# Sparse layer of a four-layer network: compression keys and key sets computed by rows with the values and then turned, and every engine's list in a new order

## The chip, the cores and the metric

One core of one Trainium2 chip runs the whole kernel. The metric is the device time of one execution in microseconds (us). The time before is 866.23 us, the median of 3 runs (866.14 to 866.57).

## The reference, cut to what matters

The reference is a whole network on one sequence of 256 rows of 1024 numbers, all float32: an even layer (top-k sparse attention and retention), an odd layer (differential and low-rank attention), a "sparse" layer with compressed, selected and window attention, and a layer with block attention over shared keys; the last two are each followed by a convolutional feed-forward network. The change touches the arithmetic of the sparse layer alone:

```
q, kc, vc, ks, vs, kw, vw, g, qm = split_cols(x @ a_w_in, sizes)   # 768, 6 x 64, 36, 256 columns
k_cmp = nsa_compress(heads(kc), pe_k, w1_k, w2_k)   # 15 blocks of 32 rows, through a small network
v_cmp = nsa_compress(heads(vc), pe_v, w1_v, w2_v)
gates = sigmoid(g)
o_main = nsa_attention(q, k_cmp, v_cmp, ks, vs, kw, vw, gates, rel_bias)
o_mem = memory_attention(qm, mem, w_mem_kv)
x = layer_norm(ALPHA * x + concat(o_main, o_mem) @ w_out, ln1_g, ln1_b)
```

## The kernel before, in words

**Precision.** Float32 accuracy is kept with the faster fp32r form: each weight and each input is cut into a high part (`whi`, `thi`) and the rest (`wlo`, `tlo`), and a product is three matmuls: high by high, low by high, high by low. ScalarE (ACT) makes the high part of a weight unit (L762), VectorE (DVE) the rest (L769). Of weight units that are split there are 262, of at most 128x1024 numbers, loaded in a fixed order by SyncE (SP, L736) into 4 raw buffers and split into 6 pairs of high and low buffers; a unit's `hi` waits until the unit six before it has been used for the last time.

**Two kinds of linear.** A "tile" (`pe_tile` L787, `pe_tile_low` L803) has 128 weight columns as the stationary operand and all 256 rows as the moving one, so its result comes out turned (columns on the partitions). For most names the high pass takes 512 moving columns at once (L797: rows' high and low parts side by side); for `e_idx` and `a_c` it takes two matmuls of 256 (L800, L801). The low pass is L809. A "chunk" (`pe_chunk` L847, `pe_chunk_low` L866) has 128 rows of the input as the stationary operand (q is 0 or 1) and the weight columns as the moving one, so its result comes out by rows: L861 (high by high), L864 (low by high), L872 (high by low). Both kinds end in one of PSUM's 8 banks, handed out in turn (`in_turn`, L629); in the sparse layer linears use banks 0 and 1 in turn. `p.fill` lets TensorE (PE) wait until the bank's last reader is done.

**The sparse layer's first linears.** `a_v` is a chunk linear of 164 columns (128 of values, 36 of gates) in 2 weight units: 8 slices of the contraction, 2 row blocks, 3 passes, so 48 matmuls of 164 columns. DVE copies the values (`vsw`, L2059), ACT takes the exponential of the gates (`gte`, L2028). `a_c` is two tiles of 128 columns (keys and values for compression; the two key sets): 2 x 24 matmuls of 256 columns. ACT copies each tile in four pieces (L2019 to L2023). Then follow the tiles `a_qm` and `a_q` and the compression (`w1`, L1964, `comp1`, `comp3`, `cmps`, `cmp`, `cmpt`).

**Attention.** Each group of heads goes through `log` (scores, L1062, into banks 4 and 5, both of them for every group), `mask` (DVE, L1179 or L1175, which empties the banks), `exp` (ACT, L1191), `mul` (DVE, L1210), `turn` (transposes, L1071), `pt` (ACT and DVE copies), and `val` (probabilities by values: L1119, and L1101 for the differential groups; in the sparse layer L1112 comes first). Most `log` steps use 64 of the 128 partitions of the stationary side, with two halves of the array side by side; `val` steps other than the differential ones use 64 of the array's columns, again two halves side by side. The `log` steps of the groups l0 to l2 use the full array. Below, "half-array steps" means the first two; `score`, `rets`, `brow`, `w1` and `cmps` (L1603, L1614 to L1633, L1964, L1997) likewise use a part of the array.

**Other steps on PE.** `T` turns the layer's input (L905), `proj` and `plow` are the output projection (L973), `mix` L932, `uq` and `ukv` L1789 to L1813, `jt` L2151, and `up`, `ulow`, `down` in the feed-forward network L2161, L2169, L2189.

**What sets the order.** The table `ORDER` (L241) holds for each of seven sections (start, even, odd, nsa, ffn0, moba, ffn1) one list of steps for each of PE, ACT, DVE and POOL, written out in the file. Each engine runs its list strictly in order; semaphores do the rest. `hi n` on ACT and `lo n` on DVE split the next n weight units.

Of the kernel before, what the change touches and what calls it, by code (L numbers as in the profile page):

```python
# [235 lines left out]
def listed(text):  # L236
# [21 lines left out]
        T 1 1 0, T 1 1 1, chunk e_av 0 0, clow e_av 0 0, chunk e_av 1 0, clow e_av 1 0, chunk e_av 0 1, clow e_av 0 1, chunk e_av 1 1,  # L258
        clow e_av 1 1, chunk e_av 2 0, clow e_av 2 0, chunk e_av 2 1, clow e_av 2 1, chunk e_av 3 0, chunk e_av 3 1, clow e_av 3 0,
        clow e_av 3 1, tile e_idx 0, tile e_idx 1, tile e_idx 2, tlow e_idx 0, tlow e_idx 1, tlow e_idx 2, tile e_rot 0, tlow e_rot 0,  # L260
        tile e_rot 1, tlow e_rot 1, iw, score 0, tile e_rot 2, tlow e_rot 2, score 1, tile e_rot 3, tlow e_rot 3, chunk e_bv 0 0,
        chunk e_bv 1 0, clow e_bv 0 0, clow e_bv 1 0, chunk e_bv 0 1, clow e_bv 0 1, tile e_q 0, chunk e_bv 2 0, chunk e_bv 1 1,
        chunk e_bv 2 1, clow e_bv 1 1, clow e_bv 2 0, clow e_bv 2 1, chunk e_bv 3 0, chunk e_bv 3 1, clow e_bv 3 0, tlow e_q 0,
        clow e_bv 3 1, tile e_q 1, tlow e_q 1, tile e_q 2, tlow e_q 2, rets 0, brow, tile e_q 3, tlow e_q 3, tile e_k 0, tlow e_k 0,
        rets 2, retv 0, retv 1, tile e_k 1, tlow e_k 1, retv 2, retv 3, tile e_k 2, tile e_k 3, tlow e_k 2, tlow e_k 3, tile e_ag 0,
        tile e_ag 1, log d0, tlow e_ag 0, tlow e_ag 1, tile e_ag 2, log d1, chunk e_bg 0 0, tile e_ag 3, tlow e_ag 2, tlow e_ag 3,
        clow e_bg 0 0, chunk e_bg 1 0, clow e_bg 1 0, turn d0 0, turn d0 1, log d2, chunk e_bg 2 0, chunk e_bg 3 0, chunk e_bg 0 1,
        clow e_bg 0 1, chunk e_bg 1 1, turn d1 0, turn d1 1, clow e_bg 1 1, val d0, chunk e_bg 2 1, chunk e_bg 3 1, val d1, turn d2 0,
        turn d2 1, clow e_bg 2 0, clow e_bg 3 0, clow e_bg 2 1, clow e_bg 3 1, val d2, proj e 0 1, proj e 1 1, proj e 0 0, plow e 0 0,
# [2 lines left out]
        proj e 4 1, proj e 5 1, plow e 4 1, plow e 5 1, proj e 6 1, plow e 6 1, proj e 7 1 0, T 3 0 0, proj e 7 1 1, T 3 0 1"""),
        act=listed("""
        T 1 1 0, T 1 1 1, hi 4, chunk e_av 0, hi 1, chunk e_av 1, rot 0, hi 3, tile e_idx 0, hi 1, tile e_idx 1, tile e_idx 2, hi 2,
        rot 1, half e_rot 0, half e_rot 1, relu 0 0, relu 0 1, hi 3, half e_rot 2, relu 1 0, relu 1 1, half e_rot 3, hi 3, chunk e_bv 0,
        hi 1, chunk e_bv 1, hi 2, half e_q 0, half e_q 1, half e_q 2, hi 2, half e_q 3, half e_k 0, half e_k 1, hi 3, half e_k 2,
        half e_k 3, hi 3, half e_ag 0, half e_ag 1, exp d0 0, exp d0 1, hi 1, half e_ag 2, half e_ag 3, exp d1 0, exp d1 1, hi 1, pt d0,
        exp d2 0, exp d2 1, silu e, brow, pt d1, out d0, out d1, pt d2, chunk e_bg 0, hi 1, chunk e_bg 1, hi 1, out d2, hi 3, mix e 2,
        mix e 3, hi 3, sq post0 0 0, sq post0 0 1, hi 1, sq pre1 0 0, sq pre1 0 1, hi 2, sq post0 1 0, T 3 0 0, sq post0 1 1, T 3 0 1,
        hi 1, sq pre1 1 0, sq pre1 1 1, hi 1"""),  # L280
        dve=listed("""
        T 1 1 0, T 1 1 1, lo 2, rt 0 0, rt 0 1, lo 2, rt 0 2, lo 1, rt 1 0, lo 4, rt 1 1, lo 1, rt 1 2, lo 1, iw, sum e_rot 0, score 0, rt 2 0,
        sum e_rot 1, lo 3, sum e_rot 2, sum e_rot 3, score 1, top 0, top 1, lo 3, top 2, top 3, top 4, lo 1, sum e_q 0, top 5, lo 1,
        sum e_q 1, sum e_q 2, dec 0, top 6, dec 1, lo 2, sum e_k 0, top 7, dec 2, sum e_q 3, dec 3, topmask, lo 1, sum e_k 1, lo 2,
        rstat 0, sum e_k 2, sum e_k 3, rstat 1, rout 0, mask d0 0, brow, mask d0 1, sum e_ag 0, sum e_ag 1, lo 3, mask d1 0, mul d0,
        mask d1 1, rout 1, sum e_ag 2, sum e_ag 3, mask d2 0, mask d2 1, pt d0, mul d1, lo 1, mul d2, pt d1, gated d0, lo 1, outlo d0,
        gated d1, pt d2, outlo d1, lo 1, gated d2, lo 1, gate e 0, gate e 1, outlo d2, lo 4, mix e 2, mix e 3, lo 3, gain post0 0 0,
        gain post0 0 1, xw e 0 0, xw e 0 1, lo 1, row pre1 0 0, row pre1 0 1, gain post0 1 0, T 3 0 0, gain post0 1 1,
        T 3 0 1, xw e 1 0, xw e 1 1, lo 1, row pre1 1 0, row pre1 1 1, lo 1"""),
        pool=listed("""  # L290
        rope 0, rope 1, rope 2, rope 3, rroot 0, rroot 1, rms post0 0, rms pre1 0, rms post0 1, rms pre1 1""")),
    odd=dict(
        pe=listed("""
        chunk o_lora 0 0, clow o_lora 0 0, chunk o_lora 1 0, chunk o_v 0 0, clow o_lora 1 0, chunk o_lora 2 0,
        chunk o_lora 3 0, clow o_lora 2 0, T 3 1 0, chunk o_v 1 0, T 3 1 1, chunk o_lora 0 1, clow o_lora 0 1, chunk o_lora 1 1,
# [2142 lines left out]
```

## Time and profile before

| | before |
|---|---|
| median of 3 runs | 866.23 us |
| span of the profiled execution | 864.6 us |
| PE busy | 855.4 us, 99% |
| PE weight loads busy | 725.5 us, 84% |
| DVE busy | 671.9 us, 78% |
| ACT busy | 489.5 us, 57% |
| POOL busy | 40.3 us, 5% |
| DMA | 155.12 MB, mean 179 GB/s |

The profile has no time of its own for the profiled execution other than its span, from the first to the last instruction; the rest of a run's time lies around the span. PE matmuls overlap, so a busy PE is not yet a PE at its best: the useful number is the distance from the start of one step to the start of the next, which the chain of waits gives (start, length, engine and line, count).

### The profile page before, as it was taken

The page shows a single profiled execution, that of the slowest core. Times are in us where ns is not written, and L with a number is a line of the kernel's source. Part 1 is how long each engine was busy: PE and PEld are TensorE (multiplying, and loading weights), DVE is VectorE, ACT ScalarE, POOL GpSimd, SP SyncE. Part 2 cuts the span into 40 slices and gives each one's busy share as a digit, 9 for nine tenths or more (in the row PEclk, how much of TensorE's full clock was granted, in tenths as well). Part 3 has the DMA queues.
Part 4 walks back from the last instruction along what each step waited for, and adds up shares of the span by engine and source line. Part 5 has one row for each costly group of instructions (what it writes and reads, how often), then busy time and mean ns, then how long its engine had stood idle before and what let it go on. Part 6 is the DMA issues. An engine that isn't in the chain of part 4 may idle for free.

```text
span 864.6 us, 13438 instructions
## 1 busy us (share of the span) xinstructions
PE 855.4 (99%) x5062; PEld 725.5 (84%) x5062; DVE 671.9 (78%) x1238; ACT 489.5 (57%) x905; POOL 40.3 (5%) x72
## 2 busy tenths in 40 slices
PE   9999999999999999999999999999999999999997
PEld 7888888888888878788888888888888888888885
DVE  4889887868886788988776867887768787677876
ACT  5584375668775776655555445545664565544541
POOL 0105000110001100000000000000000000000000
PEclk9999999999999999999999999999999999999999
DMA  9775526467436861235566556537344456566641
GB/s 328 287 240 150 167 80 194 137 221 222 167 99 228 268 219 49 77 111 179 172 202 212 174 193 228 188 131 251 115 159 146 146 195 221 169 220 213 216 155 49
DMA packets 46748, 155.12 MB, mean 179 GB/s; under 512 B 5500, under 2 KB 8668, under 8 KB 46684
## 3 DMA queue, kind: packets, MB, share of 16 engines
q1 hardware_dynamic: 41408, 141.39, 48.9%
q10 hardware_dynamic: 5276, 12.88, 4.9%
q8 instruction: 40, 0.66, 0.3%
q14 instruction: 24, 0.20, 0.1%
HBM read 152.38 MB, written 1.34 MB: 178 GB/s over the span
## 4 chain that ended last, share of the span: by engine, by line
PE 97%; DVE 1%; ACT 1%; DMA 0%; issue 0%; SPq 0%; POOL 0%; DVEq 0%
PE ps L2161 17%; PE ps L2189 14%; PE ps L797 12%; PE ps L973 10%; PE ps L2169 9%; PE ps L809 6%; PE ps L861 5%; PE ps L872 4%; PE ps L864 4%; PE ps L1062 4%; PE ps L1119 3%; PE ps L1071 3%; PE ps L905 1%; PE ps L800 1%; PE ps L801 1%; DMA raw<-in_ws 0%
## 5 line engine op out<-in xcount | busy, mean ns | idle before, releaser
L769 DVE TENSOR_TENSOR wlo<-raw,whi 128x1024 fp32r<-128x1024 f32 (+1 forms) x262 | 311.1, 1216 | 56.6 <-ACT whi L762 55.3
L762 ACT ACTIVATE whi<-raw 128x1024 fp32r<-128x1024 f32 x261 | 266.6, 1049 | 115.9 <-DMA raw<-in_ws 37.1
L2161 PE MATMUL ps<-t,whi 128*128 128x512 f32 x640 | 156.1, 391 | 0.0
L2161 PEld LDWEIGHTS ps<-t,whi 128*128 128x128 f32 x640 | 117.7, 188 | 22.8
L797 PE MATMUL ps<-t,whi 128*128 128x512 f32 x432 | 109.3, 397 | 0.0
L2189 PE MATMUL ps<-whi,r 128*128 128x512 f32 x352 | 95.4, 391 | 0.0
L797 PEld LDWEIGHTS ps<-t,whi 128*128 128x128 f32 x432 | 78.2, 188 | 17.3 <-issue 1.8
L2169 PEld LDWEIGHTS ps<-t,wlo 128*128 128x128 f32 x640 | 84.7, 191 | 4.7
L2169 PE MATMUL ps<-t,wlo 128*128 128x256 f32 x640 | 86.4, 283 | 0.0
L2189 PEld LDWEIGHTS ps<-whi,r 128*128 128x128 f32 x352 | 64.6, 188 | 12.2
L809 PEld LDWEIGHTS ps<-t,wlo 128*128 128x128 f32 (+1 forms) x472 | 62.5, 189 | 4.2 <-issue 0.3
L809 PE MATMUL ps<-t,wlo 128*128 128x256 f32 (+1 forms) x472 | 64.8, 283 | 0.0
L861 PE MATMUL ps<-whi,t 128*128 128x512 f32 (+3 forms) x192 | 56.2, 379 | 0.8 <-ACT whi L760 0.6
L2189 PE MATMUL ps<-wlo,r 128*128 128x512 f32 x176 | 54.9, 390 | 0.0
L864 PE MATMUL ps<-whi,t 128*128 128x512 f32 (+3 forms) x192 | 54.3, 371 | 0.1
L872 PE MATMUL ps<-wlo,t 128*128 128x512 f32 (+3 forms) x192 | 49.7, 371 | 0.0
L1191 ACT ACTIVATE sm<-sm,stat 128x128 f32<-128x128 f32 (+1 forms) x92 | 40.4, 442 | 5.6 <-DVE stat L1179 5.6
L825 ACT ACTIVATE arena<-ps 128x256 f32<-128x256 f32 x50 | 18.5, 380 | 41.9 <-PE ps L809 41.6
L861 PEld LDWEIGHTS ps<-whi,t 128*128 128x128 f32 x192 | 33.1, 188 | 8.1 <-issue 1.3
L864 PEld LDWEIGHTS ps<-whi,t 128*128 128x128 f32 x192 | 34.2, 188 | 6.8 <-DVE t L917 1.0
L2189 PEld LDWEIGHTS ps<-wlo,r 128*128 128x128 f32 x176 | 33.0, 188 | 7.0
L872 PEld LDWEIGHTS ps<-wlo,t 128*128 128x128 f32 x192 | 33.7, 188 | 5.8 <-issue 0.3
(277 smaller groups left out, 1149.4 us busy)
## 6 DMA issues: line engine op xcount, KB each, us to landing
raw<-in_ws SPq DMA_DIRECT2D x251, 512.0 KB, 4.5
vecs<-in_vecs ACTq DMA_DIRECT2D x12, 512.0 KB, 4.6
arena<-in_ws ACTq DMA_DIRECT2D x5, 512.0 KB, 7.5
raw<-in_ws SPq DMA_DIRECT2D x8, 256.0 KB, 5.6
raw<-in_ws SPq DMA_DIRECT2D x4, 416.0 KB, 4.3
tb<-brow ACTq DMA_DIRECT2D x8, 192.0 KB, 4.3
rows<-in_mem SPq DMA_DIRECT2D x4, 256.0 KB, 5.2
x<-in_x SPq DMA_DIRECT2D x1, 1024.0 KB, 7.6
```

What stands on the lines that cost most here:

```text
L762: a.i.activation(whi[:, j % NSPLIT, 0:n], raw[:, j % NRAW, 0:n], ACT.Copy).then_inc(*a.sig("hi", u))
L769: d.i.tensor_tensor(wlo[:, j % NSPLIT, 0:n], raw[:, j % NRAW, 0:n], whi[:, j % NSPLIT, 0:n].bitcast(F), ALU.subtract).then_inc(*d.sig("lo" ...
L797: p.i.matmul(ps[:, b, :], wh[:, k, :], t2[:, k, :], start=k == 0, stop=False)
L809: mm = p.i.matmul(ps[0:m, b, 0:T], wl[:, k, :], thi[:, k, :], start=False, stop=k == 7)
L861: p.i.matmul(chunk_out(name, b, n), thi[:, k0 + kl, q * P:q * P + P], wh[:, kl, :], start=k == 0 and kl == 0, stop=False)
L864: p.i.matmul(chunk_out(name, b, n), tlo[:, k0 + kl, q * P:q * P + P], wh[:, kl, :], start=False, stop=False)
L872: mm = p.i.matmul(chunk_out(name, b, n), thi[:, k0 + kl, q * P:q * P + P], wl[:, kl, :], start=False, stop=final and kl == nk - 1)
L973: mm = p.i.matmul(ps[:, 2 * q + z, :], x_, w_[:, 0, 512 * z:512 * z + 512], start=n == 0 and y == 0, stop=y == 2 and n + 1 in (8, add), sk ...
L1191: ex = a.i.activation(o, i, ACT.Exp, bias=g.m[:, s * n + c:s * n + c + 1], scale=1.0 if g.kind == "mem" else -1.0, accum_out=g.l[:, l:l + 1])
L2161: p.i.matmul(ps[:, b, :], wh[:, k, :], t2[:, k, :], start=k == 0, stop=False)
L2169: mm = p.i.matmul(ps[:, b, 0:T], wl[:, k, :], thi[:, k, :], start=False, stop=k == 7)
L2189: mm = p.i.matmul(ps[:, 2 * q + n, :], g_, w_[:, 0, 512 * n:512 * n + 512], start=False, stop=final and y == 2, skip_group_check=True)
```

## The change

The 256 columns of `a_c` join the 164 of `a_v`: one chunk linear of 420 columns in 4 weight units of 840 numbers a partition. ACT copies the 256 new columns of each row block to `crows` (which lies in `hrow`), and PE turns them with four transposes of 128x128 into bank 0, where the four-piece copies find them. All lists are in a new order. SP loads the same bytes in the same number of units.

```diff
-    chunk("a_v", a, span(960, 64) + span(1088, 64) + span(1152, 36))
-    tiles("a_c", a, span(768, 128) + span(896, 64) + span(1024, 64))
+    chunk("a_v", a, span(960, 64) + span(1088, 64) + span(1152, 36) + span(768, 128) + span(896, 64) + span(1024, 64))
...
+    N["crows"] = N["hrow"].rearrange("p (q n) -> p q n", q=2)
...
-                   a_v=164, b_v0=512, b_v1=256, f_in0_0=512, f_in1_0=512)
+                   a_v=420, b_v0=512, b_v1=256, f_in0_0=512, f_in1_0=512)
...
-    in_turn(*both("a_v"), *each("a_c"), *each("a_qm"), *each("a_q"), n=2)
+    in_turn(*both("a_v"), "a_c", *each("a_qm"), *each("a_q"), n=2)
...
+            elif name == "a_v":
+                p.fill(b, ("ev", "a_v", q), ("crows", q))
...
+            elif what == "crows":
+                b = BANK["a_c"]
+                p.fill(b, ("ev", "a_c", 0), ("ev", "a_c", 1))
+                for q in range(2):
+                    p.wait_ge("crows", q)
+                    for t in range(2):
+                        mm = p.i.transpose(ps[:, b, t * T + q * P:t * T + q * P + P], N["crows"][:, q, t * P:t * P + P], ident[:, :])
+                mm.then_inc(*p.sig("c_turned", 0))
...
-                pv = ps[:, BANK["a_c", t], 0:T]
-                a.wait_ge("lin", "a_c", t)
+                pv = ps[:, BANK["a_c"], t * T:t * T + T]
+                a.wait_ge("c_turned", 0)
...
+            elif what == "crows":
+                q = k[0]
+                a.wait_ge("evd", "a_v", q)
+                a.i.activation(N["crows"][:, q, :], ps[:, BANK["a_v", q], 164:420], ACT.Copy).then_inc(*a.sig("crows", q))
```

Of the lists, those parts that the prediction speaks of. PE, start:

```diff
-        warm 6 7, T 0 0 0, warm 3 7, chunk mv 0 0, T 0 1 0, clow mv 0 0, chunk mv 0 1, clow mv 0 1, T 0 0 1, T 0 1 1, chunk mv 1 0, chunk mv 1 1,
+        warm 6 7, T 0 0 0, warm 3 7, chunk mv 0 0, T 0 1 0, clow mv 0 0, T 0 0 1, chunk mv 1 0, chunk mv 0 1, clow mv 0 1,
+        T 0 1 1, clow mv 1 0, chunk mv 2 0, chunk mv 1 1, chunk mv 3 0, chunk mv 3 1, chunk mv 2 1, clow mv 1 1, clow mv 2 0,
+        clow mv 3 0, clow mv 2 1, clow mv 3 1, tile mk0 0, tile mk0 1, tlow mk0 0, tlow mk0 1, tile mk1 0, tlow mk1 0,
```

PE, sparse layer (nsa), in its first half:

```diff
-        chunk a_v 0 0, clow a_v 0 0, chunk a_v 1 0, clow a_v 1 0, T 5 1 0, T 5 1 1, chunk a_v 0 1, chunk a_v 1 1, clow a_v 0 1,
-        clow a_v 1 1, tile a_c 0, tlow a_c 0, tile a_c 1, tlow a_c 1, tile a_qm 0, tlow a_qm 0, tile a_qm 1, tlow a_qm 1, w1 k 0, w1 k 1,
-        w1 k 2, log m0, tile a_q 0, tile a_q 1, log m1, tlow a_q 0, tlow a_q 1, turn m0 0, turn m0 1, w1 k 3, w1 v 0, w1 v 1, w1 v 2,
-        w1 v 3, log n0, tile a_q 2, tlow a_q 2, log n1, comp1, tile a_q 3, tlow a_q 3, turn m1 0, turn m1 1, log n2, val m0, comp3,
-        tile a_q 4, tlow a_q 4, val m1, turn n0 0, turn n0 1, tile a_q 5, tlow a_q 5, turn n1 0, log n3, cmps, proj a 0 0, cmp,
...
+        chunk a_v 0 0, chunk a_v 1 0, clow a_v 0 0, clow a_v 1 0, T 5 1 0, chunk a_v 3 0, chunk a_v 2 0, T 5 1 1, chunk a_v 0 1,
+        clow a_v 2 0, clow a_v 3 0, chunk a_v 3 1, chunk a_v 1 1, clow a_v 0 1, chunk a_v 2 1, clow a_v 1 1, clow a_v 2 1,
+        clow a_v 3 1, crows, tile a_qm 0, tlow a_qm 0, tile a_qm 1, tlow a_qm 1, tile a_q 0, tlow a_q 0, log m0, w1 k 0, w1 k 1,
+        w1 k 2, w1 k 3, w1 v 0, w1 v 1, log m1, tile a_q 1, tlow a_q 1, turn m0 1, tile a_q 2, turn m0 0, tlow a_q 2, log n0,
+        val m0, w1 v 2, w1 v 3, log n1, turn m1 1, turn m1 0, comp1, log n2, tile a_q 3, tlow a_q 3, tile a_q 4, turn n0 0,
+        tlow a_q 4, turn n0 1, tile a_q 5, log n3, tlow a_q 5, comp3, log n4, val m1, cmps, turn n1 0, turn n1 1, cmp,
+        proj a 0 0, turn n2 0, plow a 0 0, proj a 1 0, plow a 1 0, proj a 0 1, log n5, turn n2 1, cmpt 0, proj a 1 1, val n0,
+        log n6, turn n3 1, cmpt 1, proj a 2 0, plow a 0 1, val n1, log n7, plow a 2 0, plow a 1 1, turn n3 0, val n2, turn n4 0,
+        proj a 2 1, plow a 2 1, turn n4 1, val n3, log n8, proj a 3 0, proj a 4 0, proj a 5 0, turn n5 0, val n4, turn n5 1,
```

ACT and DVE, the opening of the sparse layer; PE in the odd layer, in the first feed-forward network and in the last layer's attention (parts):

```diff
-        T 5 1 0, T 5 1 1, gte 0, hi 2, gte 1, hi 1, tile a_c 0, hi 1, tile a_c 1, hi 3, half a_qm 0, half a_qm 1, w1load 4, w1load 5,
+        T 5 1 0, hi 1, T 5 1 1, hi 1, gte 0, hi 1, w1load 4, crows 0, crows 1, gte 1, tile a_c 0, tile a_c 1, hi 1, half a_qm 0,
+        hi 3, half a_qm 1, w1load 5, half a_q 0, exp m0 0, exp m0 1, hi 1, w1load 6, w1load 7, exp m1 0, hi 1, half a_q 1,
...
+        T 5 1 0, lo 1, T 5 1 1, lo 1, vsw 0, lo 1, vsw 1, lo 2, sum a_qm 0, sum a_qm 1, blocks, mask m0 0, mask m0 1, lo 2,
...
-        chunk o_lora 3 0, clow o_lora 2 0, T 3 1 0, chunk o_v 1 0, T 3 1 1, chunk o_lora 0 1, clow o_lora 0 1, chunk o_lora 1 1,
+        clow o_lora 2 0, chunk o_v 1 0, T 3 1 0, T 3 1 1, clow o_lora 3 0, clow o_v 0 0, chunk o_lora 0 1, chunk o_lora 3 1,
...
-        chunk f_in0_0 2 1, clow f_in0_0 2 1, chunk f_in0_0 3 1, clow f_in0_0 3 1, jt 0, up 0 1 0, up 0 1 1, ulow 0 1 0, ulow 0 1 1,
+        chunk f_in0_0 2 1, clow f_in0_0 0 1, clow f_in0_0 2 1, clow f_in0_0 3 1, up 0 1 0, jt 0, ulow 0 1 0, up 0 1 1,
...
+        clow b_v1 0 0, tile b_q 3, chunk b_v1 0 1, tlow b_q 3, chunk b_v1 1 1, chunk b_v1 1 0, clow b_v1 0 1, tile b_k 4,
+        clow b_v1 1 0, log g3, val m3, log g4, clow b_v1 1 1, tile b_q 4, tlow b_q 4, turn g2 1, turn g2 0, tlow b_k 4,
+        tile b_k 5, tlow b_k 5, turn g3 0, tile b_q 5, turn g4 1, turn g3 1, tlow b_q 5, val g2, log g5, val g3, turn g4 0,
+        proj b 0 1, proj b 0 0, proj b 1 0, plow b 0 0, val g4, log g6, turn g5 0, plow b 1 0, proj b 2 0, turn g5 1,
```

## Rows read from the trace of the kernel before

**Rows 1.** The page: span, busy time, granted clock, chain by engine.

```profile
span 864.6 us, 13438 instructions
PE 855.4 (99%) x5062; PEld 725.5 (84%) x5062; DVE 671.9 (78%) x1238; ACT 489.5 (57%) x905; POOL 40.3 (5%) x72
...
PEclk9999999999999999999999999999999999999999
...
PE 97%; DVE 1%; ACT 1%; DMA 0%; issue 0%; SPq 0%; POOL 0%; DVEq 0%
```

**Rows 2.** Chain of waits, opening of the sparse layer: start us, length us, what, count.

```profile
282.41 0.63 PE ps L861 x6
...
285.06 0.64 PE ps L905 x4
...
286.48 1.03 PE ps L861 x6
...
289.57 0.15 PE ps L800
...
295.37 1.84 PE ps L797 x8
297.20 0.95 PE ps L809 x8
```

**Rows 3.** Chain of waits, odd layer: matmuls of 416 columns.

```profile
171.51 0.38 PE ps L861 x2
```

**Rows 4.** Timelines of DVE and ACT, opening of the sparse layer: start us, length us, instruction.

```profile
289.61 0.29 DVE L2059 COPY arena<-ps 128x128 f32<-128x128 f32 x1 [0.76 <-PE ps L872]
...
295.40 0.38 ACT L2022 ACTIVATE arena<-ps 64x256 f32<-64x256 f32 x1 [0.24 <-PE ps L809]
...
299.97 0.38 ACT L825 ACTIVATE arena<-ps 128x256 f32<-128x256 f32 x1
```

**Rows 5.** DMA view, issues by tensor: count, size of one, median us to landing.

```profile
rows<-in_ws ACTq DMA_DIRECT2D x2, 512.0 KB, 5.4
```

**Rows 6.** Chain of waits: half-array steps and what follows them.

```profile
239.75 1.16 PE ps L1062 x16
...
310.48 0.87 PE ps L1071 x8
...
324.64 1.02 PE ps L1119 x16
...
330.58 1.02 PE ps L1071 x8
...
334.84 1.09 PE ps L1062 x16
...
339.37 1.06 PE ps L1062 x8
340.43 3.44 PE ps L973 x14
```

**Rows 7.** Chain of waits, feed-forward network, at its step `jt 0`.

```profile
399.60 0.61 ACT arena L2226
...
400.25 0.66 PE ps L2151 x4
```

**Rows 8.** Timeline of PE, odd layer, at the step `T 3 1 0`.

```profile
168.29 0.66 PE L905 MATMUL ps<-ident,rows 128*128 128x128 f32 x4 [0.16 <-DVE rows L1352]
```

**Rows 9.** Chain of waits at the start, and ACT's timeline of the same stretch.

```profile
7.04 0.50 PE ps L861
...
12.45 0.47 PE ps L861 x2
...
19.27 1.06 ACT L762 ACTIVATE whi<-raw 128x1024 fp32r<-128x1024 f32 x1 [1.06 <-DMA raw<-in_ws]
```

**Rows 10.** Timeline of DVE: first and last `mask` instruction of the group n3 (16 in all).

```profile
335.98 0.29 DVE L1179 CUSTOM_DVE_ANT_0 sm<-ps,tb 128x128 f32<-128x128 f32 x1 [0.70 <-PE ps L1062]
...
337.68 0.09 DVE L1179 DVE_READ_ACCUMULATOR2_ANT stat<- 128x1 f32 x1
```

More of the change, by code:

```diff
@@ L257 @@
         pe=listed("""
[L258 to L269, printed above, removed]
@@ L275 @@
[L275 to L278, printed above, removed]
@@ L285 @@
[L285 to L288, printed above, removed]
@@ new lines @@
+        tile e_ag 2, tlow e_ag 1, tlow e_ag 2, log d1, tile e_ag 3, chunk e_bg 0 0, turn d0 0, tlow e_ag 3, clow e_bg 0 0,
+        turn d0 1, chunk e_bg 2 0, chunk e_bg 1 0, chunk e_bg 0 1, val d0, log d2, turn d1 1, turn d1 0, chunk e_bg 3 1,
+        chunk e_bg 3 0, clow e_bg 2 0, chunk e_bg 1 1, val d1, clow e_bg 1 0, clow e_bg 3 0, turn d2 0, turn d2 1,
+        clow e_bg 1 1, clow e_bg 0 1, chunk e_bg 2 1, clow e_bg 2 1, clow e_bg 3 1, val d2, proj e 0 0, plow e 0 0, mix e 2,
+        proj e 3 0, proj e 0 1, plow e 0 1, proj e 4 0, mix e 3, proj e 5 0, proj e 2 0, proj e 1 1, proj e 6 0, plow e 3 0,
@@ L290 @@
+        xw e 1 1, lo 2, row pre1 1 0, row pre1 1 1"""),
         pool=listed("""
@@ L298 @@
-        chunk o_v 3 1, l2 0, l2 1, tile o_q 0, clow o_v 3 1, tlow o_q 0, tile o_q 1, tlow o_q 1, tile o_q 2, tlow o_q 2, tile o_q 3,
-        tlow o_q 3, uq 0, uq 1, uq 2, uq 3, ukv 0, ukv 1, ukv 2, ukv 3, log l0, tile o_dg 0, tlow o_dg 0,
-        log l1, tile o_dg 1, tile o_dg 2, turn l0 0, turn l0 1, log l2, tlow o_dg 1, tlow o_dg 2, tile o_dg 3, tlow o_dg 3, tile o_k 0,
-        tlow o_k 0, val l0, turn l1 0, turn l1 1, tile o_k 1, tlow o_k 1, tile o_k 2, turn l2 0, turn l2 1, tlow o_k 2, val l1,
@@ L321 @@
[L321 to L324 removed]
+        chunk o_lora 0 0, chunk o_lora 1 0, clow o_lora 0 0, clow o_lora 1 0, chunk o_lora 3 0, chunk o_v 0 0, chunk o_lora 2 0,
@@ new lines @@
+        tile o_dg 0, tlow o_dg 0, tile o_dg 1, log l1, tlow o_dg 1, tile o_dg 2, tlow o_dg 2, tile o_dg 3, tlow o_dg 3,
+        tile o_k 0, tlow o_k 0, log l2, turn l0 0, tile o_k 2, turn l0 1, tile o_k 1, tile o_k 3, tlow o_k 1, turn l1 1,
+        tlow o_k 2, tlow o_k 3, chunk o_cg 0 0, val l0, log x0, turn l2 0, turn l1 0, chunk o_cg 0 1, chunk o_cg 2 0, val l1,
+        log x1, turn l2 1, chunk o_cg 1 0, clow o_cg 0 0, log x2, val l2, chunk o_cg 1 1, turn x0 0, clow o_cg 0 1,
+        clow o_cg 1 0, chunk o_cg 3 1, clow o_cg 2 0, clow o_cg 1 1, val x0, chunk o_cg 3 0, chunk o_cg 2 1, turn x1 0,
```

295 lines of the change are left out of this document (156 added, 139 removed).

## The prediction

> **What bounds the kernel now.** I read the page first, then the chain of waits over the whole span, then timelines where the chain leaves PE. The page says that PE is busy for 99% of the span at the full clock (the 2.4 GHz level throughout), that DVE and ACT are well below, and that the chain is PE for 97% [rows 1]. So time is won only by fewer or shorter steps on PE, or where PE stands. The chain gives the pace: a tile's high pass of 8 matmuls of 512 columns takes 1.84 us, 0.230 each, and a low pass of 8 of 256 takes 0.95, 0.119 each [rows 2]. All through the trace steps keep these paces, with two exceptions. One is a fixed loss of about 0.2 us when PE leaves a half-array step for a full-array one: after the scores of a group the next 14 matmuls of 512 columns take 3.44 us, where 14 x 0.230 is 3.22; after a `val` step 8 transposes take 1.02 us instead of 0.87. From scores straight into `val` nothing is lost (16 matmuls in 1.02, the usual length); from `val` into scores it is little (1.16 against 1.09) [rows 6]. The other is true standing still, in few places, all told some 5 us: mostly at the start, at the `T` steps and at `jt 0`, priced below.
>
> **The merged linear.** Before, from 282.41 to 295.37, 12.96 us go to `a_v`, `a_c` and eight transposes for `T` [rows 2]. 6 matmuls of 164 columns take 0.63 us, about 0.11 each, like transposes of 128 (8 in 0.87 [rows 6]); so 48 of them are 5.3. `a_c`, from 289.57 to 295.37, is 5.80 for 48 matmuls. The transposes are 8 x 0.11 = 0.88. That is 12.0; the other 0.95 is standing around the two `T` steps (the second row block's first six take 1.03 us, not 0.63 [rows 2]). After, 48 matmuls of 420 columns: 2 of 416 take 0.38 us [rows 3], and between 256 and 512 columns one more column costs 0.111 us / 256 = 0.43 ns, so 0.19 each and 9.1 in all. With 4 new transposes (0.44) and the old eight (0.88) it is 10.4. The new list puts two chunks of q = 0 between the two `T` steps and more q = 0 work ahead of them, so I take the 0.95 as gone. Without new waits: 12.96 - 10.4 = 2.5 us won.
>
> By a rule, the columns alone would be worth nothing: the Trainium skill, "TensorE: Matmul & The Clock Gate", section "Back-to-back issue gap", gives for a single warm matmul N / 2.4 + 2.5 ns, so 71 ns at 164 columns, and then the sum over the columns, the same before and after, would leave only 48 x 2.5 ns. This trace's rows speak against it at 164 columns: 0.105 to 0.11 us, as at 128.
>
> **New waits at `crows`.** Its transposes of q = 1 follow directly on the last low pass of `a_v`, and their data go PE, DVE `vsw 1`, ACT `crows 1`, PE. In the trace the same `vsw` copy starts 0.2 us after PE has gone on, and takes 0.29 [rows 4]; an ACT copy of 128x256 takes 0.38 [rows 4]; each hand-over is 0.03 to 0.04. PE resumes about 0.94 after its last low matmul has been followed; the two q = 0 transposes cover 0.22, and the first instructions after a stand cost 0.22 more (4 transposes in 0.66 instead of 0.44 after one [rows 7]). Loss: 0.9. `tile a_qm 0` may go on (bank 1 is empty when `gte 1` is done). `tile a_qm 1` needs bank 0, and so all eight ACT copies of `a_c`: 8 x 0.39 = 3.1 us from [rows 4], begun some 0.45 after the q = 1 transposes; PE's cover is `a_qm 0`, 1.84 + 0.95. Loss: 0.6 with the restart 0.8. Behind these copies on ACT wait one `hi` and `half a_qm 0`, neither of which PE needs for 2 us. Together 1.7, so the part wins 0.8 us. Bounds: 2.5 if both are hidden, 0 if ACT or DVE comes late by another 0.8.
>
> ACT's two copies replace nothing, 0.8 us on an engine with 57%; `hi` and `lo` of 4 units of 840 numbers cost what 984 + 328 + 2 x 1024 did. SP's loads are the same bytes in as many units. Free, with ACT's spare time as cover. `w1load 5` now stands behind `half a_qm 1`; 6 us of PE work lie before `w1 v 1` reads it. Such loads landed in 5.4 us in the median [rows 5], so just in time; I take 0; a landing 2 us later than the median would cost 1.5, the upper bound, and 0 is the lower.
>
> **The new order, half-array steps.** I counted in both lists where a half-array step is followed by a full one (`val n*` begins with a full one). Before: 10 in the even layer, 5 in the odd one, 21 in the sparse one, 11 in the last, 47. After: 9, 3, 15, 8, so 35. 12 x 0.2 = 2.4 us won. `val` directly followed by `log` goes from 1 to 9 places, 8 x 0.07 = 0.6 given back. Net 1.8; bounds 1.2 (0.15 each) and 2.4.
>
> **The new order, old stands.** `jt 0` now has `up 0 1 0` before it, 1.84 us of work while ACT empties the bank: the 0.67 of [rows 7] and the restart of 0.22 go, 0.9 (in the second network, where the tile already comes first, nothing is lost). `T 3 1 0` waits 0.16, restart 0.22 [rows 8]; it gets a chunk of 0.9 us in front: 0.4. At the start PE needs 5.41 us from 7.04 to 12.45 [rows 9] for 12 matmuls of 512 columns (2.7, at 0.227) and 12 transposes (1.3), so it stands 1.4. `chunk mv 1 0` and `T 0 0 1` now fill this. But a unit for `mk0` then arrived only at 19.27, ACT waiting for its DMA [rows 9], and the new ACT list sends both vector loads (512 KB each) ahead of the second half of the start. `tile mk0 1` follows `tile mk0 0` at once and would stand about 1. I take 0.4; bounds 0 and 1.4.
>
> **The new order, new stands.** Banks 4 and 5 serve every group, so a `log` waits for the `mask` of the one before. For n3 this took DVE from 335.98 to 337.77, after scores begun at 334.84 [rows 6, 10]: 2.9 us from log to log at least, and some 2.7 for a group of the second row block. The new list has `log n0, val m0, w1 v 2, w1 v 3, log n1` (3.0 us: just enough), then `turn`, `turn`, `comp1`, `log n2` (2.6, with `lo` and a `sum` on DVE in between: about 0.6 lost), and `log g3, val m3, log g4` (1.7 us, needs some 1.9: 0.3). 0.9 lost in all; bounds 0 and 3.
>
> **Sum.** 0.8 + 1.8 + 0.9 + 0.4 + 0.4 - 0.9 = 3.4 us. The profiled span of 864.6 becomes 861.2. The median of the runs is 1.6 above that span; I leave that distance alone: 866.2 - 3.4 = 862.8. The tail (last `down` to output) is in the same order.
>
> **Rivals.**
> 1. The order hides more than I see: no new stand at all (0.9 + 1.7 back) and the start in full (1.0): 862.8 - 3.6 = 859.2. For: the middle of the trace has hardly a stand in 600 us, so such lists come out on the chip as drawn. Against: the chain at `crows` has nothing to run beside it. 0.17.
> 2. What the half-array steps win is given back to DVE: half of the nine new `val`-`log` neighbours bring their `log` too early, 5 x 0.6: 865.8. For: DVE at 78%, the gap of 2.9 us. Against: most of them (n6, n7, x0, x1) have 4 us before them. 0.13.
> 3. Slower: the same at every place. Where half-array steps are put side by side (the nine and the w1 runs, ten in all), PE waits for DVE's masks, 0.6 plus 0.2 restart, and I lose the 0.9 already counted only once: 862.8 + 8 = 870.8. It decides from the point where such stands pass 5 us together, about 6 places, since 862.8 + 5.1 is 867.9. 0.07.
> 4. The merge doesn't do what it says: 48 matmuls of 420 columns cost what 48 of 164 and 48 of 256 did, less one fixed part of 9 ns each (0.119 - 256 x 0.43 ns): 0.22 us, not 0.19, so 1.5 less is won: 864.3. The straight line through 256, 416 and 512 columns speaks against it [rows 2, 3]. 0.03. It is what the skill's rule above comes to here.
>
> **How the numbers follow.** The forecast has 0.60. A measurement of this kernel can tell about 0.2%, 1.7 us, from no change: faster is below 864.5, slower above 868.0. Faster: 0.56 of the forecast, rival 1, rival 4 half, and 0.03 of rival 2: 0.78. Same: 0.15. Slower: 0.07. The range for 8 in 10 goes from 859.4, nearly rival 1, to 866.0, rival 2 and all bounds of the sum on the bad side but DVE's.
>
> **What would show it.** In the profile after: 48 matmuls of 420 columns at 0.19 us; PE idle before the `crows` transposes with ACT as releaser, and again before the second `a_qm` tile; the chain with 35 losses of 0.2 us; no wait at `jt 0`. The forecast is wrong if PE's waits for DVE at scores or for `hi` appear in number, if the start ends later than before (first `T 1` steps), or if the paces themselves change.

## The result and the profile after

The changed kernel takes 869.62 us, median of 4 runs (869.22 to 871.08), beside 866.19 for the kernel before on the same chip: a ratio of 1.0039, 95% interval 1.0025 to 1.0053. Forecast were 862.8 us and a range from 859.4 to 866.0. It is slower, by about 3.4 us (0.4%), where 3.4 us less were forecast; the profiled execution, 869.22 us, has a span of 867.4, 2.8 more than before.

The page, with the lines that answer to [rows 1]:

```profile
span 867.4 us, 13345 instructions
PE 853.3 (98%) x5018; PEld 722.4 (83%) x5018; DVE 665.3 (77%) x1238; ACT 493.3 (57%) x909; POOL 43.2 (5%) x72
...
PEclk9999999999999999999999999999999999999999
...
PE 89%; DVE 3%; ACT 2%; DMA 2%; POOL 2%; issue 1%; SPq 0%; ACTq 0%; DVEq 0%
```

PE has less to do (853.3 us, 855.4 before) at the same clock, and the span is longer. In the chain PE held 97% and holds 89%; DVE and ACT have more of it than the 1% each of before, and DMA, GpSimd (POOL) and `issue` had nothing. These shares say who stands in the path, not what it costs: 8% of the span are 69 us, and the span grew by 2.8. The price is in PE's own waits.

The waits of PE in the changed kernel (line, releaser, us in total, times, longest):

```profile
PE ps L1081 <- DMA arena<-arena: 2.4, 1, 2.4
...
PE ps L1992 <- ACT arena L2059: 0.6, 1, 0.6
PE ps L1081 <- DVE stat L1198: 0.5, 1, 0.5
PE ps L1645 <- POOL arena L1783: 0.5, 1, 0.5
...
PE ps L814 <- ACT arena L2050: 0.5, 1, 0.5
```

L1081 is the scores of a `log` step (L1062 before), L1992 the transposes of `crows`, L1645 the scores of `rets 0`, L814 the high pass of a tile (L797). The waits for ACT were forecast, and one for DVE at a `log`, though at another step. The waits for a DMA and for GpSimd no line of the forecast names.

The opening of the sparse layer, PE's timeline, answers to [rows 2]:

```profile
293.68 0.54 PE L880 MATMUL ps<-whi,t 128*128 128x420 f32 x2
294.06 0.54 PE L883 MATMUL ps<-whi,t 128*128 128x420 f32 x2
294.44 1.30 PE L891 MATMUL ps<-wlo,t 128*128 128x420 f32 x6
295.57 0.38 PE L1992 MATMUL ps<-ident,arena 128*128 128x128 f32 x2
296.53 0.44 PE L1992 MATMUL ps<-ident,arena 128*128 128x128 f32 x2 [0.58 <-ACT arena L2059]
296.72 2.07 PE L814 MATMUL ps<-t,whi 128*128 128x512 f32 x8
298.63 1.11 PE L826 MATMUL ps<-t,wlo 128*128 128x256 f32 x8
300.23 2.08 PE L814 MATMUL ps<-t,whi 128*128 128x512 f32 x8 [0.48 <-ACT arena L2050]
```

From start to start, two matmuls of 420 columns take 0.38 us, the forecast's 0.19 each. The four transposes take from 295.57 to 296.72, 1.15 us instead of 0.44: 0.7 lost (0.9 forecast). Tile `a_qm 1` follows 1.60 after the low pass before it began, where 0.95 is the pace: 0.65 lost (0.8 forecast).

**Where the time went.** I cut PE's timeline of each kernel at the first matmul of each section (first `T 1 0 0`, first 416-column matmul, first `a_v`, first chunk of each feed-forward network and of the block layer; the last section ends with the span). Under the old lists a section's length repeats within 0.1 us from kernel to kernel, in the even layer within 0.3. Under the new ones the start moves between 31.1 and 32.7, the sparse layer by 0.8 and the odd one by 0.8, once by 1.4, the first network by 0.5, once by 1.3. For some of this the traces show why: at the start PE waits up to 1.6 us for the DMA of `rows`, and in two kernels the granted clock falls for some us (below, e3 and e5). The rest I did not trace. The forecast column spreads the sum of 3.4 over the sections:

```
section        before   after   change   forecast
start           31.80   31.42    -0.38     -0.4
even           130.66  132.00    +1.34     -0.2
odd            119.79  121.94    +2.15     -0.7
sparse         105.33  104.74    -0.59     -0.9
1st network    185.42  185.71    +0.29     -0.9
block          101.08  100.78    -0.30     -0.3
2nd network    190.52  190.81    +0.29      0
```

Start, sparse and block layer came near the forecast; for the first two that says little, since their own spread is larger. Most of the error, 6.2 us between the two spans, is in the odd layer (2.9), the even layer (1.5) and the first network (1.2).

### The profile page after: what moved, and what is told of

Read it like the earlier page. It is cut to its first block, busy times and chain, and to the rows that moved or that the text cites. A ratio compares the mean times of both kernels' runs of the same rounds, so it can differ in the third digit from the quotient of the medians.

```text
span 867.4 us, 13345 instructions
## 1 busy us (share of the span) xinstructions
PE 853.3 (98%) x5018; PEld 722.4 (83%) x5018; DVE 665.3 (77%) x1238; ACT 493.3 (57%) x909; POOL 43.2 (5%) x72
## 4 chain that ended last, share of the span: by engine, by line
PE 89%; DVE 3%; ACT 2%; DMA 2%; POOL 2%; issue 1%; SPq 0%; ACTq 0%; DVEq 0%
PE ps L2192 17%; PE ps L2220 14%; PE ps L814 10%; PE ps L992 10%; PE ps L2200 9%; PE ps L826 6%; PE ps L891 4%; PE ps L880 4%; PE ps L883 4%; PE ps L1081 3%; PE ps L1138 2%; PE ps L1090 2%; PE ps L924 1%; DMA arena<-arena 1%; POOL arena L1780 1%; DMA raw<-in_ws 1%
## 5 line engine op out<-in xcount | busy, mean ns | idle before, releaser
L786 DVE TENSOR_TENSOR wlo<-raw,whi 128x1024 fp32r<-128x1024 f32 (+2 forms) x262 | 311.9, 1212 | 58.8 <-ACT whi L779 57.3
L814 PE MATMUL ps<-t,whi 128*128 128x512 f32 x432 | 108.6, 395 | 0.5 <-ACT arena L2050 0.5
L814 PEld LDWEIGHTS ps<-t,whi 128*128 128x128 f32 x432 | 78.0, 188 | 16.5 <-issue 1.0
L826 PEld LDWEIGHTS ps<-t,wlo 128*128 128x128 f32 (+1 forms) x456 | 60.0, 189 | 4.0 <-issue 1.0
L880 PE MATMUL ps<-whi,t 128*128 128x512 f32 (+3 forms) x192 | 57.9, 385 | 0.5 <-ACT whi L777 0.5
L883 PE MATMUL ps<-whi,t 128*128 128x512 f32 (+3 forms) x192 | 56.0, 376 | 0.2 <-DVE t L936 0.2
```

The lines of the kernel that those rows point to most:

```text
L786: d.i.tensor_tensor(wlo[:, j % NSPLIT, 0:n], raw[:, j % NRAW, 0:n], whi[:, j % NSPLIT, 0:n].bitcast(F), ALU.subtract).then_inc(*d.sig("lo" ...
L814: p.i.matmul(ps[:, b, :], wh[:, k, :], t2[:, k, :], start=k == 0, stop=False)
L826: mm = p.i.matmul(ps[0:m, b, 0:T], wl[:, k, :], thi[:, k, :], start=False, stop=k == 7)
L880: p.i.matmul(chunk_out(name, b, n), thi[:, k0 + kl, q * P:q * P + P], wh[:, kl, :], start=k == 0 and kl == 0, stop=False)
L883: p.i.matmul(chunk_out(name, b, n), tlo[:, k0 + kl, q * P:q * P + P], wh[:, kl, :], start=False, stop=False)
```

## The experiments

**`krep` early (e1).** `krep`, a DMA of 512 KB, lies in ACT's list; the new list has it behind `uq 0`, `uq 1`, `tbl 0`.

```diff
-half o_q 3, uq 0, uq 1, tbl 0, krep, uq 2,
+half o_q 3, krep, uq 0, uq 1, tbl 0, uq 2,
```

> The changed kernel with one step moved in ACT's list of the odd layer: krep (the copy of the rotated keys by DMA) ahead of uq 0 again, where the old list had it. Theory A, the step's DMA is issued 4.2 us later by the new list, behind three evictions, and log l0 waits for it: the wait of PE on DMA at log l0 falls from 2.4 us to 0.4 or less, the odd section (119.8 us before, 121.9 changed) comes back to 119.6 to 120.1 us, and the time is 867.2 to 867.7 us. Theory B, the odd section lost its time to its new order in general (stands spread over many steps), and behind that wait stands another at the same place: the section gives back 0.5 us or less, the time is 869.1 us or more.

867.52 us, 1.0015 of before (1.0005 to 1.0025). The odd section is 119.58, 2.36 shorter. The rows behind it, from ACT's timeline (the issue; before, then changed, then this kernel) and from PE's timeline of the changed kernel:

```profile
197.56 0.72 ACTq L1831 DMA_DIRECT2D arena<-arena  x1
```

```profile
201.15 0.63 ACTq L1844 DMA_DIRECT2D tb<-brow  x1
201.81 0.69 ACTq L1850 DMA_DIRECT2D arena<-arena  x1
...
209.57 2.02 PE L1081 MATMUL ps<-arena 128*128 128x128 f32 x16 [2.41 <-DMA arena<-arena]
```

```profile
199.37 0.72 ACTq L1850 DMA_DIRECT2D arena<-arena  x1
```

The copy lands 7.6 us after its issue at 201.81; PE is at `log l0` 2.4 us earlier. Issued ahead of the evictions, its landing, 8.3 us by the DMA view, is just covered. Theory A holds; B falls, since no other stand took the place.

The late issue is half of it. The DMA view's row of this copy, before, changed, this kernel (the last figure is the time to landing):

```profile
arena<-arena ACTq DMA_DIRECT2D x1, 512.0 KB, 5.5
```

```profile
arena<-arena ACTq DMA_DIRECT2D x1, 512.0 KB, 7.6
```

```profile
arena<-arena ACTq DMA_DIRECT2D x1, 512.0 KB, 8.3
```

At 5.5 us the copy issued at 201.81 would have landed at 207.3, some 0.15 us after PE got there (an estimate from these rows). So the stand of 2.4 us needs both: 2.6 us less between the issue and PE's arrival (8.0 before, 5.35 changed), and 2.1 us more to land. In all five kernels with the old list of the odd layer the copy takes 5.5 to 5.7 us; in the eight with the new one whose traces have the usual pace (all but e10), 6.1 to 8.8. With the new list the copies into `tb` (`tbl 0`, `tbl 1`) are on their way at the same time; with the old one they are issued after the landing (before: 204.69, landed 203.06). That they slow it down fits all thirteen traces, but no run moves them alone, so it is argued and not shown.

**Old lists for even and odd (e3).** Only the lists of these two sections are the old ones.

> The changed kernel with the old lists of the even and of the odd layer; everything else, the merged linear too, is the changed kernel's. Theory A, the loss lies in these two sections (1.3 and 2.1 us by the two traces) and the rest is worth what the traces of its sections say (start -0.4, sparse -0.6, first feed-forward +0.4, block layer -0.4, second feed-forward +0.3): 865.5 to 866.5 us, 0.999 to 1.0005 of before. Theory B, the sections are coupled by the transfers of weights and buffers, and the old lists bring new waits to the later sections: 867.5 us or more.

866.94 us, 1.0002 (0.9992 to 1.0011); even 130.91, odd 119.73, sparse 104.86, first network 185.79. The even and the odd section have their old lengths and the others stay near the changed kernel's, so the two lists carry the loss and no new wait came with them: theory A by the sections. The time is 0.4 above its bound. In the profiled execution the start took 32.71, 1.3 more than in the changed kernel: PE waited 2.0 us for a `hi`, and from 7.7 to 11.0 the granted clock was 0.50, the 1.2 GHz level, where the changed kernel has 1.00. Whether that explains the median of the other runs no trace shows.

**The merge alone (e4).** Old lists everywhere, the merged linear put into the sparse one by hand.

```diff
-T 5 1 0, T 5 1 1, gte 0, hi 2, gte 1, hi 1, tile a_c 0, hi 1, tile a_c 1, hi 3,
+T 5 1 0, hi 1, T 5 1 1, hi 1, gte 0, hi 2, crows 0, crows 1, gte 1, tile a_c 0, tile a_c 1, hi 3,
```

> The kernel before with the merge alone: keys for compression and the two key sets in the linear of values and gates (420 columns), turned by crows in the place where their two tiles stood; every list otherwise the old one. By the prediction's first term (2.5 us of PE work saved, 1.7 us of waits at crows and behind it) the sparse section gets 0.8 us shorter, 104.4 to 104.8 us against 105.3, and the time is 865.4 us. Rival, the matmul with 420 columns costs more than its share (0.19 to 0.22 us each in place of 0.18) or the waits hold all that is saved: the section is 105.2 us or more, the time 866.1 us or more.

868.72 us, 1.0026 (1.0015 to 1.0038). The sparse section is 107.56, 2.2 longer than before, where I expected 0.8 less. PE's timeline:

```profile
294.16 0.63 PE L1976 MATMUL ps<-ident,arena 128*128 128x128 f32 x4 [1.38 <-ACT arena L2043]
...
298.05 2.08 PE L798 MATMUL ps<-t,whi 128*128 128x512 f32 x8 [0.48 <-ACT arena L2034]
...
303.53 0.70 PE L1065 MATMUL ps<-kmT,arena 64*128 64x256 f32 x4 [1.01 <-DVE arena L835]
```

and ACT's:

```profile
291.74 2.00 ACT L763 ACTIVATE whi<-raw 128x1024 fp32r<-128x1024 f32 x2 [1.45 <-PE ps L875]
293.65 0.64 ACT L2043 ACTIVATE arena<-ps 128x256 f32<-128x256 f32 x2
```

The matmuls are as short as in the changed kernel. But both copies of the rows stand behind two `hi` of 1.0 us, the sum that `log m0` needs comes late, and `w1` waits 0.4 for its weights. The rival's bound holds, by far more than I expected: the merge is worth what the queues beside it allow. No kernel has the new lists without the merge, so the reverse isn't measured.

**The merge with ACT's and DVE's lists laid for it (e9).** As e4, but `gte 0`, `w1load 4` and `crows` ahead of the second `hi`, and DVE's sums of `a_qm` ahead of `gate0`.

> As e4 (old lists, merge alone, 107.56 us for the sparse section), with ACT's and DVE's lists from T 5 1 0 to a_qm in the changed kernel's manner: gte 0, w1load 4 and crows ahead of the second hi, the sums of a_qm ahead of gate0, PE's list unchanged. Theory A, e4 lost 1.4 us at crows, 0.5 behind it, 1.0 at log m0 and 0.4 at w1 because its queues were not laid for the merge: the section is 105.0 to 105.6 us. Theory B, the waits are the chain's own length: 107 us or more.

One run, 867.44 us; the section is 106.59. Not half of the way: the wait at `crows` is 0.4 us and that for DVE is gone, but `log m0` now waits 0.7 for ACT, and PE stands 0.7 at a `w1` for something that the view doesn't name. Between the two theories; neither range held.

**`crows` behind a tile (e5).** On the changed kernel: the turned rows get bank 2, and PE turns them behind the high pass of `a_qm 0`.

```diff
-clow a_v 3 1, crows, tile a_qm 0, tlow a_qm 0,
+clow a_v 3 1, tile a_qm 0, crows, tlow a_qm 0,
-gte 1, tile a_c 0, tile a_c 1, hi 1, half a_qm 0, hi 3, half a_qm 1,
+gte 1, tile a_c 0, half a_qm 0, tile a_c 1, hi 4, half a_qm 1,
```

> The changed kernel with the turned rows put in a third bank of PSUM and crows moved behind the products of tile a_qm 0, on ACT the first eviction of a_qm between the two of a_c: PE has 2.2 us of work while ACT writes the rows. Theory A, the stand at crows (0.6 us) and the one at the tile behind it (0.5 us) are waits for ACT and go: the sparse section falls from 104.7 to 103.4 to 103.8 us, the time to 868.4 to 868.8 us. Theory B, the work of ACT and DVE behind these places is the bound and the stand moves to log m0: 0.3 us or less are won.

A miss, 872.14 us, 1.006 (1.0045 to 1.0075). Both stands are gone, but the section is 105.26, for a reason of my own making:

```profile
PE ps L814 <- DVE arena L851: 2.4, 1, 2.4
```

`sum a_qm 0` stood on DVE behind a `lo`, which waited for the `hi` that I had moved back. The odd section, not touched, was 123.37 here, 1.4 longer than in the changed kernel, and not by waits: the stand at `log l0` is again 2.4 us, but the 16 matmuls behind it take 3.23 us from start to start of the next step, 1.78 in the changed kernel. From 209.5 to 211.4 the granted clock was 0.50 (the 1.2 GHz level), in the changed kernel 1.00. So of the 872.14 about 1.4 us belong to neither theory.

**The same, DVE's sum ahead (e6).** `krep` is early as well.

```diff
-gte 1, tile a_c 0, half a_qm 0, tile a_c 1, hi 4, half a_qm 1,
+gte 1, tile a_c 0, half a_qm 0, hi 1, tile a_c 1, hi 3, half a_qm 1,
-vsw 1, lo 2, sum a_qm 0, sum a_qm 1,
+vsw 1, lo 1, sum a_qm 0, lo 1, sum a_qm 1,
```

> As e5 (crows behind the products of tile a_qm 0, turned rows in a third bank), with krep early as in e1, and with DVE's sum a_qm 0 ahead of the lo it stood behind, one hi on ACT between the first half of a_qm and the second eviction of a_c. In e5 the stand at crows was gone, but PE then waited 2.4 us for sum a_qm 0. Theory A, that wait was the queue's doing (sum behind lo behind hi): without it the sparse section is 102.8 to 103.6 us (104.7 in the changed kernel), the time 866.0 to 866.7. Theory B, ACT's eight copies have to be paid somewhere between a_v and log m0: 104.4 us or more, the time 867.4 or more.

867.74 us, 1.0016 (1.0007 to 1.0026); the section is 104.57. It looks like theory B: the stand has moved to `log m0`. ACT's timeline says why:

```profile
299.98 1.06 ACT L780 ACTIVATE whi<-raw 128x1024 fp32r<-128x1024 f32 x1
...
300.95 1.98 ACT L780 ACTIVATE whi<-raw 128x1024 fp32r<-128x1024 f32 x2
302.96 0.66 ACT L843 ACTIVATE arena<-ps 128x256 f32<-128x256 f32 x2
```

```profile
PE ps L1082 <- DVE arena L852: 1.7, 1, 1.7
```

The half that `log m0` waits for comes behind three `hi`. That is an order, not a full engine, and can be tried. Of the time, two things lie outside the sparse section: the copy of `krep` took 8.8 us to land and PE waited 0.5 for it in spite of the early issue, and the first network was 186.87, 1.2 above the changed kernel's, in part by a wait of 0.4 for a `hi`.

**`jt 0` and three exits (e7).** The kernel before with two edits in two sections.

```diff
-clow f_in0_0 3 1, jt 0, up 0 1 0, up 0 1 1,
+clow f_in0_0 3 1, up 0 1 0, jt 0, up 0 1 1,
...
-log g2, val m2, chunk b_v1 0 0, tile b_q 3,
+log g2, chunk b_v1 0 0, val m2, tile b_q 3,
...
-log g4, val m3, tile b_q 4, tlow b_q 4,
+log g4, tile b_q 4, val m3, tlow b_q 4,
...
-log g6, val g4, plow b 0 0, plow b 1 0,
+log g6, plow b 0 0, val g4, plow b 1 0,
```

> The kernel before with two edits, read by sections of its profile. In the first feed-forward network up 0 1 0 is put ahead of jt 0 and nothing else is changed: by the prediction the section (185.42 us) loses 0.9; if the stand there was only what the step's own length shows (1.26 us for 8 transposes that take 0.88), 0.4. In the block layer three val steps that follow scores directly are parted from them by one full-array step each: at 0.2 us for each time PE leaves a half-array step, the section (101.08 us) gets 0.6 longer; rival, the loss belongs to something else in those places: 0.1 or less.

One run, 867.73 us. The first network became 185.22, 0.20 shorter, not 0.9. Its stand at `jt 0` is gone, but a low pass further on, 0.95 us elsewhere, takes 1.13 from start to start:

```profile
407.20 1.11 PE L2169 MATMUL ps<-t,wlo 128*128 128x256 f32 x8
408.33 1.86 PE L2161 MATMUL ps<-t,whi 128*128 128x512 f32 x7
```

The block layer became 102.90, 1.82 longer. Two of the three added exits stand free of other changes: from `log g2` to the end of the next high pass the same work takes 5.21 us instead of 4.98, and at `log g6` 4.70 instead of 4.49. The third, at `log g4`, lies in one place with a new stand (0.94 us of waiting for DVE at a transpose, and what restarting costs), and the two together are 1.4. The place at `log g6`, PE's timeline before and then with the edit:

```profile
646.69 1.13 PE L1062 MATMUL ps<-arena 64*128 64x256 f32 x8
647.75 1.09 PE L1119 MATMUL ps<-pt,arena 128*64 128x128 f32 x16
648.78 1.20 PE L973 MATMUL ps<-wlo,r 128*128 128x512 f32 x4
...
651.18 0.60 PE L1071 MATMUL ps<-ident,sm 128*128 128x128 f32 x4
```

```profile
647.60 1.14 PE L1062 MATMUL ps<-arena 64*128 64x256 f32 x8
648.66 0.73 PE L973 MATMUL ps<-wlo,r 128*128 128x512 f32 x2
649.33 1.09 PE L1119 MATMUL ps<-pt,arena 128*64 128x128 f32 x16
...
652.30 0.60 PE L1071 MATMUL ps<-ident,sm 128*128 128x128 f32 x4
```

The same work takes 4.49 us and then 4.70. The exit at 0.2 us stands as priced, by two places. Fewer of them is a gain, then, but not when the order that saves them puts a stand elsewhere.

**`rets 0` later (e8).** On the changed kernel with early `krep`:

```diff
-tile e_q 1, tile e_q 3, tlow e_q 1, rets 0, tlow e_q 3, tile e_q 2, tlow e_q 2, rets 2,
+tile e_q 1, tile e_q 3, tlow e_q 1, tlow e_q 3, tile e_q 2, tlow e_q 2, rets 0, rets 2,
```

> The changed kernel with krep early and, in PE's list of the even layer, rets 0 moved 2.8 us later, behind tile e_q 2. Theory A, PE waits there for GpSimd's rope (0.5 us and 0.15 of restart): the even section falls from 132.0 to 131.3 to 131.5 us. Rival, the wait belongs to the chain behind the rope and is found again at retv 0 or at turn d0: less than 0.2 us won.

A bad miss: one run, 872.34 us, the even section 137.80. The wait for GpSimd is gone, and PE waits for DVE at `rets 2`:

```profile
PE ps L1645 <- DVE sm L1734: 4.0, 1, 4.0
```

`rets 2` needs the two banks that `dec 0` and `dec 1` empty, and with `rets 0` moved nothing was left between the two. DVE, whose list has `dec 0` ahead of `top 4` and the sums, stood idle for 4.5 us in front of it. Here to delay PE's step did not cure the late supplier; it made the next step's supplier late. The section is 5.8 us longer than in e1, more than the wait. The rest goes with the clock: PE stood from 91.1 to 95.1, and from 93.8 to 100.7 the granted clock was 0.51 (the 1.2 GHz level). It is the one 8 in the page's row of the clock:

```profile
PEclk9999899999999999999999999999999999999999
```

**The rope (e10, e12).** e10 is e6 with two edits: in the even layer DVE's three `lo` are parted; in the sparse layer `half a_qm 1` comes after one `hi`. e12 is e1 with the first of them alone.

```diff
-rt 2 0, sum e_rot 3, brow, lo 3, top 0, top 1, lo 1, top 2,
+rt 2 0, sum e_rot 3, brow, lo 1, top 0, lo 1, top 1, lo 2, top 2,
-half a_qm 0, hi 1, tile a_c 1, hi 3, half a_qm 1,
+half a_qm 0, hi 1, tile a_c 1, hi 1, half a_qm 1, hi 2,
```

> The changed kernel with krep early, and two edits read by sections. Even layer: DVE's three lo steps that follow sum e_rot 3 are parted by top 0 and top 1. In the changed kernel GpSimd's first rope product takes 4.25 us (0.74 elsewhere) beside those three, and rets 0 waits for the last rope. Theory A, GpSimd's 128x256 product waits out DVE's lo steps that run back to back, whatever else is there: that product takes under 2.5 us, PE's wait at rets 0 (0.5 us, 0.67 with its restart) goes, the section falls from 132.0 to 131.3 to 131.6. Rival, the product is slow at its first use, or the ropes just start too late: nothing won. Sparse layer: as e6, with ACT's half a_qm 1 after one hi and not after three. In e6 the stand of crows came back as 1.7 us at log m0, behind that half: theory A, it is the queue's order again, the section is 102.8 to 103.6 us; theory B, ACT is full there and the stand only moves on: 104.2 us or more.

865.10 us, 0.9981 (0.9972 to 0.9991), 2.4 us less than e1, with early `krep` alone, or 2.9 by the two ratios. Its one profiled execution took 3561 us: a matmul of 512 columns had 1.1 to 1.5 us where 0.39 is usual, while DVE's and ACT's steps kept their lengths, and this trace has no record of the clock. Why is open, and the split comes from the next kernels. The rope alone:

> The changed kernel with krep early and, of the two edits of e10, the even layer's alone: DVE's three lo steps behind sum e_rot 3 are parted by top 0 and top 1. (The profiled execution of e10 took 3561 us and shows nothing of it.) Theory A, GpSimd's first rope product, 4.25 us beside three lo steps in a row, waits them out and now takes under 2.5 us; PE's wait at rets 0 goes; the even section falls from 132.0 to 131.3 to 131.6 us. Rival: the product is slow for another reason, or rets 0 waits for DVE instead: 131.9 or more.

One run, 866.40 us; even 131.64, 0.4 shorter, just outside the range. The wait at `rets 0` is gone. GpSimd's first rope product and DVE beside it, changed kernel:

```profile
71.56 4.25 POOL L1780 TENSOR_TENSOR arena<-arena,tb 128x256 f32<-128x256 f32 x1 [42.11 <-DVE arena L851]
75.77 0.73 POOL L1781 TENSOR_TENSOR arena<-arena,tb 128x256 f32<-128x256 f32 x1
```

```profile
71.72 3.48 DVE L786 TENSOR_TENSOR wlo<-raw,whi 128x1024 fp32r<-128x1024 f32 x3
75.13 0.74 DVE L1712 MAX8 arena<-arena 128x8 f32<-128x128 f32 x2
```

and with the `lo` steps parted:

```profile
71.81 1.98 POOL L1780 TENSOR_TENSOR arena<-arena,tb 128x256 f32<-128x256 f32 x1 [42.03 <-DVE arena L851]
```

```profile
71.98 1.20 DVE L786 TENSOR_TENSOR wlo<-raw,whi 128x1024 fp32r<-128x1024 f32 x1
73.11 0.74 DVE L1712 MAX8 arena<-arena 128x8 f32<-128x128 f32 x2
```

The product ends at 75.81 and DVE's row of `lo` at 75.20; then at 73.79 and 73.18: 0.61 behind the last `lo` both times. Theory A. The Trainium skill, "SBUF — State Buffer", section "SBUF: two separate sides", says it as a rule: between a DVE operation with two SBUF inputs and a GpSimd one that reads SBUF the shared port pair is an exclusive lock, and the one that starts first has it for the whole instruction. This trace agrees that one waits the other out, and shows that GpSimd did not get in between the three (3.48 us). On the order it does not agree: the product's row begins 0.16 us before the first `lo`, and yet it was the product that waited. Starts on GpSimd are rough in this view, so that is no proof against the rule.

**Two combinations (e11, e13).** The best section of either list:

> The best section of either list as measured so far: the even layer and both feed-forward networks from before (the first with up 0 1 0 ahead of jt 0, -0.2), start and block layer from the changed kernel (about 0, -0.3), the odd layer changed with krep early (-0.2 to -0.6), the sparse layer as in e10 (-1.7 to -2.5 if its theory A holds, -0.9 if not). Sum against the kernel before: -2.5 to -3.5 us in the first case, 863.0 to 864.0 us, ratio 0.996 to 0.997; -1.5 in the second, 865.0 us. If sections are coupled by transfers and buffers more than their single measurements show, 866 us or more.

863.94 us against 866.91 beside it, 0.9964 (0.9950 to 0.9978), span 861.9: even 130.90, odd 119.22, sparse 103.27, first network 185.21, block 100.69. It beats both kernels. And with the changed list of the even layer:

> The combination e11 (863.94 us, span 861.9) with the changed kernel's list of the even layer and the parted lo steps in place of the old list. If the even section comes to 131.3 to 131.6 us, it stays above the old list's 130.66 to 130.9, and the time is 864.3 to 864.8; by the times of e10 against e1 (2.9 us apart, of which the sparse section should explain some 1.1) it could be as low as 130.2, and the time 863.3 us.

864.24 us, 0.9973 (0.9964 to 0.9982), span 861.2; even 131.60, sparse 102.55. The sparse section is 2.78 shorter than before, and from 282 to 345 us PE's only wait is 0.3 at `cmp`. So `crows` can be hidden in full (theory A of e10): that gave 1.0 and 1.7 us against the 104.3 of the list with early `krep` alone, where the forecast had put 1.7 on these stands. The section's own spread of 0.8 is as large as the difference of the two. The two combinations can't be told apart by their times; the old even list has the shorter section.

## Why the prediction was wrong

The step that failed is the part on the new order. It asked of each moved step on PE what bank or mask it would wait for. It did not ask what was moved in the other queues: the part has no sentence on ACT's `krep` or `tbl`, nor on GpSimd's ropes, though both lists were in the diff. In its sum both stand at nothing; the runs show 2.4 us and 0.4 us, of an error of 6.2 between the two spans. The rest of the error is `jt 0` (0.7) and small losses whose cause is in part open. The forecast was a gain of 3.4 us and the result a loss of 3.4.

- **Odd layer, no term, 2.4 us.** `krep`'s DMA is issued behind three ACT steps; one move back and the section was 2.36 shorter. That the early issue cures it is shown. The stand also needed the longer landing, 7.6 us for 5.5, whose cause is argued only.
- **Even layer, no term, 1.3 us.** `rets 0` waited for the rope, which waited out three `lo`: 0.4 shown by parting them. The other 0.9 is spread: PE's timeline has steps 0.1 to 0.4 us over their pace at some eight places, the largest 0.38 at a `val` step that waits 0.23 for DVE. I did not test them one by one, so their cause is open.
- **`jt 0`, forecast 0.9, measured 0.2.** I read the chain's ACT piece of 0.61 in [rows 7] as PE's stand. PE was at work for most of it; its own timeline shows 0.25 us of waiting, and 0.41 with the restart. Half of that came back at a low pass. The rest of this network's new list lost another 0.5 (185.22 with the `jt` edit alone, 185.58 to 185.87 in most kernels with the whole list), in stands of 0.1 to 0.2 us. The second network lost 0.3, with no wait that a view names; its cause is open.
- **The merged linear, forecast 2.5 less 1.7: right in the changed list.** From its first matmul to `a_qm 0` the opening takes 11.36 us (285.36 to 296.72) with 0.7 of the stand in it, 12.95 before: 2.3 saved without it. 0.19 us per matmul, 0.7 and 0.65 us of stands for 0.9 and 0.8. My lower bound, 0, was wrong for the merge on its own: -2.2 in the old lists. The price belongs to the queues around it.
- **Half-array exits, 0.2 each: right**, 0.23 and 0.21 at two added ones. The count was right too: PE's timelines have 47 such places before and 35 after. The Trainium skill, "TensorEngine Tiling (Array Packing)", section "Key Properties", says that a change of tiling mode drains the engine; it gives no figure. The runs show the cost, not that a drain is behind it.
- **DVE's masks:** forecast 0.6 at `log n2` and 0.3 at `log g4`; measured 0.54 at `log n1`, which the forecast had as just enough, nothing at `log n2` and 0.10 at `log g4`. That one size is nearly met is luck, the place is wrong. Rivals 2 and 3 fell: they put the danger at the masks, and the changed kernel has one such wait above 0.1 us. Rival 1 fell with the stands at `crows`, rival 4 with the 0.19 us. The slower case came true, by another mechanism than the one I had written.
- **Start, forecast 0.4:** not found. Over all kernels the old list gives 31.3 to 31.8, the new one 31.1 to 32.7, so the -0.38 of the table is luck.
